# Merge stage of a two-block transformer forward pass: 24 of 32 gate tiles as pairs by seven products

## The reference, cut to what matters

```python
gates = jax.nn.sigmoid(p["gate"] + merge_gate_b).reshape(Bn, S, N_BRANCH, D_MODEL)
merged = (gates[:, :, 0] * y_ml + gates[:, :, 1] * y_gla
          + gates[:, :, 2] * y_conf + gates[:, :, 3] * y_sc)
return merged @ w_o
```

## Time and profile before

| | |
|---|---|
| median of 3 runs | 1973.01 us (1972.1 to 1973.63) |
| the profiled execution | 1973.15 us, span from first to last instruction 1971.2 us |
| PE busy | 1959.5 us, 99% of the span |
| PE weight loads (PEld) | 1640.5 us, 83% |
| DVE, ACT, POOL busy | 1291.6 us (66%), 893.8 us (45%), 128.4 us (7%) |
| granted PE clock, mean | 0.999 |
| transfers | 278.80 MB, mean 141 GB/s |

### The profile page before, as it was taken

The page is one execution under the profiler, slowest core; times in us unless marked ns, Lnnn a source line. Parts: engine busy times, 40 slices in busy tenths (PEclk is TensorE's granted clock), DMA queues, the critical chain, the costliest instruction groups (busy, mean ns, idle before and its releaser), DMA issues.

```text
span 1971.2 us, 29262 instructions
## 1 busy us (share of the span) xinstructions
PE 1959.5 (99%) x10404; PEld 1640.5 (83%) x10404; DVE 1291.6 (66%) x2073; ACT 893.8 (45%) x1417; POOL 128.4 (7%) x202
## 2 busy tenths in 40 slices
PE   9999999999999999999999999999999999999999
PEld 7777789898987888898998888778888888888888
DVE  6555578676687776787786679484444786653545
ACT  4555555445444554544454443564333544432333
POOL 0111011111111111000001000000000000000000
PEclk9999999999999999999999999999999999999999
DMA  5899968677666115666656313111322412232222
GB/s 200 211 232 240 203 180 204 198 188 189 221 209 150 55 50 149 199 177 186 191 178 244 110 44 106 64 65 66 106 96 96 144 43 86 95 100 103 93 93 91
DMA packets 92909, 278.80 MB, mean 141 GB/s; under 512 B 10488, under 2 KB 13560, under 8 KB 92560
## 3 DMA queue, kind: packets, MB, share of 16 engines
q1 hardware_dynamic: 67200, 187.20, 29.1%
q0 software_dynamic: 24896, 88.14, 18.8%
q10 hardware_dynamic: 720, 2.23, 0.3%
HBM read 275.39 MB, written 52.47 MB: 166 GB/s over the span
## 4 chain that ended last, share of the span: by engine, by line
PE 95%; DVE 2%; DMA 1%; ACT 1%; issue 0%; SPq 0%; DVEq 0%; ACTq 0%
PE bank L962 23%; PE bank L964 23%; PE bank L963 23%; PE bank L1285 4%; PE bank L1287 4%; PE bank L1286 4%; PE bank L1085 1%; DMA w_raw<-in_wstream 1%; PE bank L1144 1%; PE bank L1067 1%; PE bank L1160 1%; PE bank L1070 1%; PE bank L1018 1%; PE bank L1112 1%; PE bank L1020 1%; PE bank L1019 1%
## 5 line engine op out<-in xcount | busy, mean ns | idle before, releaser
L962 PE MATMUL bank<-b_hi,w_hi 128*128 128x512 f32 x2060 | 812.3, 394 | 2.7 <-DVE w_lo L3172 1.3
L964 PE MATMUL bank<-b_hi,w_lo 128*128 128x512 f32 x2060 | 802.2, 389 | 0.0
L963 PE MATMUL bank<-b_lo,w_hi 128*128 128x512 f32 x2060 | 802.0, 389 | 0.0
L962 PEld LDWEIGHTS bank<-b_hi,w_hi 128*128 128x128 f32 x2060 | 386.8, 188 | 91.1 <-issue 8.4
L964 PEld LDWEIGHTS bank<-b_hi,w_lo 128*128 128x128 f32 x2060 | 386.8, 188 | 81.1
L963 PEld LDWEIGHTS bank<-b_lo,w_hi 128*128 128x128 f32 x2060 | 387.0, 188 | 80.2 <-issue 2.4
L2835 DVE TENSOR_TENSOR w_lo<-w_raw,w_hi 128x1024 fp32r<-128x1024 f32 (+3 forms) x259 | 306.7, 1184 | 216.9 <-ACT w_hi L1879 216.0
L1879 ACT ACTIVATE w_hi<-w_raw 128x1024 fp32r<-128x1024 f32 (+3 forms) x259 | 265.6, 1025 | 285.0 <-PE bank L964 265.6
L3995 DVE SCALAR_TENSOR_TENSOR arena<-bank,vec,arena 128x511 f32<-128x511 f32 x88 | 65.7, 749 | 85.9 <-ACT arena L2729 80.6
L1285 PE MATMUL bank<-parts,w_hi 128*128 128x256 f32 x384 | 108.1, 282 | 0.1
L1287 PE MATMUL bank<-parts,w_lo 128*128 128x256 f32 x384 | 108.0, 281 | 0.0
(11 more groups left out here) (403 smaller groups left out, 2550.0 us busy)
## 6 DMA issues: line engine op xcount, KB each, us to landing
w_raw<-in_wstream SPq DMA_DIRECT2D x253, 512.0 KB, 3.5
arena<-in_ada POOLq DMA_DIRECT2D x30, 512.0 KB, 4.6
plain<-seven_sums SPq DMA_DIRECT2D x48, 256.0 KB, 5.0
early<-seven_sums SPq DMA_DIRECT2D x48, 256.0 KB, 4.2
plain<-in_wseven SPq DMA_DIRECT2D x36, 256.0 KB, 4.7
early<-in_wseven SPq DMA_DIRECT2D x36, 256.0 KB, 5.3
plain<-in_ada POOLq DMA_DIRECT2D x18, 512.0 KB, 4.4
seven_sums<-in_wseven POOLq DMA_DIRECT2D x16, 512.0 KB, 5.2
```

Source lines behind the costliest of these rows:

```text
L962: nc.tensor.matmul(dst, whi, rhs_hi(k), start=(k == 0), stop=False)
L963: nc.tensor.matmul(dst, whi, rhs_lo(k), start=False, stop=False)
L964: last = nc.tensor.matmul(dst, wlo, rhs_hi(k), start=False, stop=(k == n - 1))
```

## The change

The gate tiles of j = 2 to 7 (24 of 32) are computed as 12 pairs (branches 0 and 1, and 2 and 3, of each j) by seven products each; those of j = 0 and 1 stay as they are. With that:

- The weights' sums of the 12 pairs are made in DRAM by 36 further transfers on GpSimd's queue, 24 ahead of the memset of `gla_w`, and then 3 and 9. Each handles two pairs: copies of 1 MB, additions of 512 KB.
- The inputs' sums need the input at full precision, which is no longer stored; GpSimd adds its high and low parts (`whole`, eight additions), DVE makes the sums (`gate_sums`), ACT their high part, DVE their low part.
- SP no longer streams whole panels in the merge, but groups of two quarters (256 KB each) from the weights or their sums, through a ring of four buffers; the branch panel of j - 1 is the fifth of the eight groups of j.
- PE, ACT and DVE run the six blocks j = 2 to 7 by orders that are written out: 14 products and, after the eighth, the branch tiles of j - 1.
- A product's bank is copied or added into the gate tile in halves of 256 tokens (ACT `gate_set`, `last_gate_set`; DVE `gate_add`), and the sigmoid is applied when the tile is complete (`gates_out`).
- The squares of x use other tiles of the arena.

The core of the diff:

```diff
-    ("merge", (BRANCHES + 1) * KT), ("w_o", KT), ("ffn2", 2 * HID_T + 3 * KT),
+    ("merge", 2 * BRANCHES + 2), ("w_o", KT), ("ffn2", 2 * HID_T + 3 * KT),
...
 # SP
+            def load_gates(j, q):
+                group, raw = gate_group(j, q), gate_raw(j, q)
+                if group >= 4:
+                    r = q - 4
+                    sp.wait_ge(seven_lo, item_count(j if r >= 0 else j - 1,
+                                                    BRANCH_ITEM if r % KT == 4 else item(2 * (r % KT) + (1 if r % KT < 4 else -1))))
+                elif group % 2:
+                    sp.wait_ge(head_lo, 4)
+                else:
+                    sp.wait_ge(w_lo_done, PANEL0["merge"] + (KT if group == 0 else KT + 1))
...
+            for j in range(2, KT):
+                sp.wait_ge(sum_in, gate_sums_made(j))
+                for q in range(KT):
+                    load_gates(j, q)
...
 # GpSimd
+            gate_parts(0, 24)
             pool.wait_ge(head_h, 2)
             for w in gla_w:
                 pool.memset(w, 0.0).then_inc(pads_set, 1)
+            whole(0)
+            gate_parts(24, 3)
+            whole(2)
+            gate_parts(27, 9)
...
 # PE
+            def gate_products(j, u):
+                q, o = u // SEVEN, u % SEVEN
+                n = unit(j, q)
+                chain = s_bank[n % 2]
...
+                pe.wait_ge(seven_lo, item_count(j, item(u)))
+                if n == 0 and o == 0:
+                    pe.wait_ge(gate_done, 2 * BRANCHES)
+                if n == 0 and o == 1:
+                    pe.wait_ge(mixed_low, MIXED_LOW0 + 2 * UNITS + QUAD)
...
             branch_tiles(0, 0)
-            merge_tile(2, 0)
-            merge_tile(3, 1)
-            with pe.Fori(2, KT // 2) as jj:
-                merge_tile(2 * jj, 0)
-                merge_tile(2 * jj + 1, 1)
+            for j in range(2, KT):
+                for u in range(GATE_U * SEVEN):
+                    gate_products(j, u)
+                    if u == KT - 1:
+                        pe.wait_ge(seven_lo, item_count(j, BRANCH_ITEM))
+                        branch_tiles(j - 1, 1)
+            panel_ready(g0 + 2 * BRANCHES + 1)
             branch_tiles(KT - 1, 1)
...
 # ACT
+            gate_sums_high(0)
+            gate_sums_high(1)
             squares(3, c_bank[:], gla_e[1][0], 2)
...
             for n in range(EARLY - 2):
                 act.wait_ge(gate_early, n + 1)
                 act.activation(early_gate[n], early_gate[n], ACT.Sigmoid).then_inc(gate_done, 1)
+                if n == EARLY - 4:
+                    gate_sums_high(2)
...
+            gate_high(2, 0)
+            gate_high(2, 1)
+            gate_sums_high(3)
+            gate_high(2, 2)
+            gate_high(2, 3)
+            for j in range(2, KT):
+                gate_set(j, 0)
+                gate_high(j, 4)
+                gate_set(j, 1)
+                gate_high(j, 5)
+                gate_set(j, 2)
+                gate_high(j, 6)
+                gate_high(j, 7)
+                if j == 2:
+                    merged_high(0, 0)
+                branch_high(j)
+                last_gate_set(j, 6)
...
+                if j < KT - 1:
+                    merged_high(j - 1, (j - 1) % 2)
+                    for u in range(3):
+                        gate_high(j + 1, u)
+                    last_gate_set(j, 13)
+                    gate_high(j + 1, 3)
+                else:
+                    act.wait_ge(seven_mm, products_done(j, 11))
+                    split(half0 + BRANCHES, 1, PANEL, None)
+                    last_gate_set(j, 13)
+                    w_o_split(0, None)
+                gates_out(j, 13)
...
 # DVE, behind the last head_low
+            dve.wait_ge(head_lo, 4)
+            gate_sums(2)
+            gate_low(2, 0)
+            gate_low(2, 1)
+            gate_sums(3)
+            gate_sums_low(2)
+            gate_sums_low(3)
+            branches(0, 0, lambda: (gate_low(2, 2), gate_low(2, 3)))
+            for j in range(2, KT):
...
+                gate_add(j, 5)
+                gate_low(j, BRANCH_ITEM)
+                gate_low(j, 9)
+                gate_low(j, 10)
+                branches(j - 1, (j - 1) % 2, lambda: (gate_low(j, 11), gate_low(j, 12)))
+                gate_low(j, 13)
+                gate_low(j, 14)
+                if j < KT - 1:
+                    merged_low(j - 1, (j - 1) % 2)
+                x_sums(j - 2, j % 2)
+                gate_add(j, 10)
+                gate_add(j, 11)
+                if j < KT - 1:
+                    gate_low(j + 1, 0)
+                    gate_low(j + 1, 1)
+                gate_add(j, 12)
+                if j < KT - 1:
+                    gate_low(j + 1, 2)
+                    gate_low(j + 1, 3)
+                else:
+                    split(half0 + BRANCHES, 1)
```

More of the change, by code:

```diff
@@ L782, in _, with load_rest @@
             base += (MIX0 - PANEL0["mla_out"]) * P * PANEL
[L783 to L787, removed]
+            def load_rest(first, last, at):
+                with sp.Fori(0, (last - first) // 2) as half:
+                    for s in range(2):
+                        load(s, 2 * half + (first + s), (2 * half + s) * (P * PANEL) + at, PANEL)
+                return at + (last - first) * P * PANEL
@@ new lines, in _ @@
+            merge = PANEL0["merge"]
+            base = load_rest(MIX0, merge + KT, base)
+            load(0, merge + KT, base, PANEL)
+            for j in range(2, KT):
+                sp.wait_ge(sum_in, gate_sums_made(j))
+                for q in range(KT):
+                    load_gates(j, q)
+            sp.wait_ge(seven_lo, item_count(KT - 1, BRANCH_ITEM))
+            load(1, merge + KT + 1, base + P * PANEL, PANEL)
+            sp.wait_ge(seven_lo, item_count(KT - 1, item(11)))
+            last = N_PANELS - KT
@@ L788, in _ @@
+            base = load_rest(merge + KT + 2, last, base + 2 * P * PANEL)
             width = FFN2_CHUNKS[-1] * P
@@ L3835, in branches @@
                     if b == 2:
-                        if not (isinstance(j, int) and j < 2):
+                        if j >= 2:
                             dve.wait_ge(merge_hi, j - 1)
@@ L3840, in branches @@
                         both = steps.mark(dve.tensor_tensor(merged[m], gate_at(j, m, 0), gate_at(j, m, 1), ALU.add))
+                if between is not None:
+                    between()
                 dve.wait_ge(branch_read, 4 * j + 3)
@@ L3858, in x_sums @@
                     dve.tensor_tensor(ssum_x, ssum_x, sq_x[m], ALU.add).then_inc(res_sum, 1)
-            def merge_tile(j, jj, m):
-                for p in range(5):
-                    i = 5 * m + p - 1
-                    split(5 * jj + (half0 + i // 2), i % 2)
-                    if p == 0:
-                        branches(j - 2, m)
-                    if p == 1:
-                        merged_low(j - 2, m)
-                    if p == 3:
-                        x_sums(j - 2, m)
-            merge_tile(2, 1, 0)
@@ new lines, in _ @@
+            dve.wait_ge(head_lo, 4)
[6 more added lines that the diff above has]
+            branches(0, 0, lambda: (gate_low(2, 2), gate_low(2, 3)))
+            for j in range(2, KT):
+                gate_low(j, 4)
+                gate_low(j, 5)
+                gate_low(j, 6)
+                gate_add(j, 3)
+                gate_low(j, 7)
+                gate_add(j, 4)
+                if j == 2:
+                    merged_low(0, 0)
+                gate_add(j, 5)
[17 more added lines that the diff above has]
+                    gate_low(j + 1, 3)
+                else:
+                    split(half0 + BRANCHES, 1)
```

265 lines of the change are left out of this document (194 added, 71 removed).

## The result

The changed kernel takes 1975.28 us (median of 20 executions, 1972.27 to 1979.38), the kernel before on the same chip 1972.74: ratio 1.0014, 95% interval 1.0007 to 1.0020. It is 2.5 us slower where 5.5 us faster was forecast. The profiled execution has a span of 1972.7 us against 1971.2.

What follows compares the result with a forecast made beforehand. TensorE (PE), busy 99% of the span with 95% of the last chain, was taken as the bound; -10.8 for the pairs, +2.55 and +2.25 at the entry, +0.45 at the end gave -5.5: 1967.5 us, range 1962.5 to 1973.5.

Steps and rivals of the forecast that it cites:

- The work on PE: Merge: twelve pairs at 9.98 us replace 24 gates, 119.8 against 130.6 us, a gain of 10.8 us.
- GpSimd's queue: Weight-sum transfers ahead of the gla_w memset: four blocks of 50 us end at 1296, before 1315, and cost nothing.
- Sums of the input: Ahead of the merge: eight GpSimd additions at 1.27 us, with DVE's first sums in its idle time, cost nothing.
- Rival 4: From 1316.3 to 1321.4 GpSimd's additions hold up DVE by up to 5.1 us; 1.8 cover, +3.3, 1970.8 us; chance 0.05.
- The entry: Start of the merge's first block: PE stalls 2.55 us before product 1 and 2.25 before product 2, +4.8 us.
- A block in steady state: Each merge block lasts 25.4 us, ACT and DVE fit, nothing is lost; upper bound 0.9 us a block.
- three narrow places: In each block: branch_high after product 5 (0.25 us spare), product 13's add (0.4), product 2's gate_set 0 (0.4 or 0.2).
- The end: Last block: DVE splits the last branch panel behind product 12's add, 1.9 us against product 13's 1.43, +0.45 us.
- rival 3: The granted clock falls at the entry's two stalls: +1.7 us once, 1969.2, or twice, 1970.9; chance 0.10.

Runs made afterwards that it cites:

- experiment 7: Changed kernel with GpSimd's additions moved, and 30 instead of 24 weight-sum transfers ahead of the gla_w memset: 1968.01 us, ratio 0.9973 to the kernel before.
- experiments 1: Changed kernel with GpSimd's eight additions of the input's parts replaced by memsets of the same tiles: 1967.76 us, ratio 0.9976 to the kernel before.
- experiment 3: Changed kernel with GpSimd's first four additions moved to where DVE is idle, the last four behind DVE's reads of the first sums: 1967.63 us, ratio 0.9975.
- experiment 4: Changed kernel with another order on DVE at the entry into the merge, and one exchange on ACT: 1967.48 us, ratio 0.9971 to the kernel before.
- experiment 5: Changed kernel with both the moved GpSimd additions and the new DVE order at the entry: 1963.06 us, ratio 0.9949 to the kernel before.
- experiment 12: Changed kernel with all its waits, PE running unread matmuls (19 and 12) in the two waits at the entry: 1972.13 us, ratio 1.0000 to the kernel before.
- experiment 9: Changed kernel with only the first four GpSimd additions moved to where DVE is idle: 1969.83 us, ratio 0.9984 to the kernel before.
- experiment 11: Changed kernel with moved additions, new DVE entry order and earlier last branch-panel split, GpSimd's remaining nine sum transfers held back until gate_high(2,3): 1963.10 us, ratio 0.9948.
- experiments 1 to 4: Changed kernel with additions as memsets, 1967.76 us; kernel before plus four unread additions, 1976.99; changed kernel with additions moved, 1967.63; with DVE's entry reordered, 1967.48.

## Why the prediction was wrong, point by point

**The work on PE: right.** 12 x 9.98: the blocks are 25.43 us apart (19.96 + 5.47) with seven products of 1.426. All 10.8 us came.

**GpSimd's queue: right.** The first 24 transfers took 7.98 us apart ((1280.44 - 1096.86) / 23; 8.3 was forecast), the memset stayed at 1315.7, and experiment 7 shows room for six more.

**Sums of the input: the step that failed.** "Eight additions on GpSimd at 1.27 us" was costed at nothing, with the contention put among the rivals at 0.05. They took 1.6 us, stretched four DVE operations from 2.5 to 6.9 us and made two waits of PE, 3.1 and 1.4 us with what hangs on them. Two mistakes lie in it. Rival 4 named the wrong cover: the masked copy with 1.8 us, where the split of a weight panel, further ahead in the same queue, had 1.4. That its 3.3 us is near the 3.1 of the first wait is luck: DVE was held up by 4.4 us and not by 5.1. And for the second set the forecast saw no rival at all: it laid the additions "near 1362 to 1367" and DVE's sums and low parts into the same stretch, each at its undisturbed length, though a half of the additions starts as soon as gate_sums has read the half before and so runs beside DVE by its own waits. By experiments 1 and 3, which agree, the place of the additions cost 7.7 us, the clock's share included. The rule of the Trainium skill that the prediction cited (GPSIMD Engine Reference, 8. Key points: GpSimd contends with VectorE instructions of two SBUF inputs) holds here: 0.69 us became 1.77.

**The entry: right in place, in releaser and in size.** 2.55 + 2.25 = 4.8 us were forecast. In experiment 3, where the clock is full, the 96 matmuls take 16.35 us against the 11.54 of experiment 4: 4.8. Experiment 4 shows that the order on DVE made both. One term beside them was covered by luck: the load of group 1 was to land in 5 us, and in experiment 5 ScalarE could use it only 9.3 us after it was asked for; the stall had hidden it.

**A block in steady state: right.** None of the three narrow places opened. **The end: right**, 0.4.

**The clock: rival 3, given 0.10, happened**, and in its size: 1.7 to 3.4 us were forecast at the entry, where the profiled execution lost 2.8 and experiment 12 gives back 2.8. It was tied to the entry alone; the two waits that the forecast missed added to it, and all of the changed kernel's executions have a clock of 0.996 to 0.998. The Trainium skill says there (TensorE: Matmul & The Clock Gate, Part 1) that a PE that is not busy enough falls to half rate. Experiment 12 bears it out, but in the profiled executions of experiments 1 and 3 the same two stalls left the clock at 1.00, so a stall is a risk here and not a certainty.

**The sum, made anew** from the two profiled executions, whose spans differ by 1.5 us: -10.8 for the pairs, +0.4 for the end, +4.0 of idle time at the entry, +4.5 for the two waits ahead, +0.4 that was there before the additions, and +3.1 for the clock. Of this, 2.8 is at the entry (18.18 - 11.4 - 4.0), and 0.3 ahead of it, where the fall at 1328 cost 1.6 us and took the place of the one at 1340.60, which cost the kernel before 1.3. That makes 1.6. Over all executions the difference is 2.5 us and not the 1.4 of the profiled ones (1974.56 - 1973.15), because these differ by 0.0017 in the mean clock (6.8 us more at half rate, in 1972) and all of them by 0.0027. So of the 8.0 us between forecast and result the waits ahead of the merge are 4.5 and the clock most of the rest. With both causes out (experiment 5) the kernel takes 1963.06 us, 10.2 below before (interval 7.3 to 12.6), and it beats both kernels; that this is near the 10.4 that the pairs leave after the end's 0.4 is in part the luck named in experiment 5.

**Left open:** by what rule the falls add up. Experiment 9 contradicts the rule of the three stalls, experiments 3 and 4 together a fixed price for each, and the executions of one kernel differ among themselves.

## What to carry to other kernels

An operation on an idle engine is free only if it does not slow the busy one beside it: before GpSimd work that reads SBUF is placed, see what DVE runs in that stretch and how much cover each result in DVE's queue has, not only the one that the change touches. Short waits of a saturated TensorE cost more than their length in this kernel (a wait of 3.1 us brought 5.9 when it went, experiment 9), so its order is worth settling to the microsecond; matmuls that nobody reads, put into the waits at the entry, gave back the clock's part. A transfer that is only held back can meet other loads later, as it may have done in experiment 11.

## What the runs showed of the hardware that was not expected

- One DVE operation with two SBUF inputs (128x512): 0.63 us beside GpSimd memsets, 1.04 beside copies, 1.72 beside additions. GpSimd's addition itself: 1.26 us beside an idle DVE (5.03 / 4), 1.6 beside a busy one. A low part with 1024 elements took 2.25 instead of 1.22 (experiment 3). A DVE operation with one input from PSUM kept its length in the kernel before, beside GpSimd's subtractions from 697.50 to 700.03:

```profile
698.87 0.69 DVE L3431 SCALAR_TENSOR_TENSOR b_lo<-bank,b_hi 128x512 fp32r<-128x512 f32 x1 [0.99 <-ACT b_hi L2281]
```

- Executions of one and the same kernel differ in the granted clock: beside experiments 1 to 4, 12 of the kernel before with a mean of 1.0 took 1972.1 us on average, 9 with 0.999 took 1973.5.
- Transfers that accumulate 512 KB in DRAM or copy 1 MB came 7.6 to 8.0 us apart on the mean, far less than twice the 5.2 to 6.8 us that half the size takes from issue to landing; a load of 256 KB beside such a transfer could be used after 9.3 us instead of 5 (experiment 5).
